# Attention stage of a two-block layer on Trainium2: all scores of a step ahead of the transposes of the step before, and one maximum over three PSUM banks

## The reference

```
def gqa_block(q_blk, k, v):
    s = jnp.einsum('bkgqd,bksd->bkgqs', q_blk, k).astype(jnp.float32) * (HEAD_DIM ** -0.5)
    p = jax.nn.softmax(s, axis=-1)
    return jnp.einsum('bkgqs,bksd->bkgqd', p.astype(v.dtype), v)
...
# first_block: rmsnorm, projection, Fourier branch and attention branch (each gated), output projection, residual, rmsnorm
# second_block: rmsnorm, projections, causal stick-breaking attention, causal convolution, gated merge, then a gated feed-forward part of width 2816
```

## Time and profile before

| what | value |
|---|---|
| median of 3 runs | 2025.19 us |
| the profiled execution | 2023.87 us, its span 2021.9 us |
| PE busy in the span | 1984.7 us (98%) |
| DVE, ACT, POOL busy | 1269.9, 998.3, 771.9 us |
| granted TensorE clock | 0.998 |
| attention stage | from about 262 to about 505 us of the span |
| chain that ended last | 84% PE, 9% DVE, 2% ACT |

### The profile page before, as it was taken

The page is one execution under the profiler, slowest core; times in us unless marked ns, Lnnn a source line. Parts: engine busy times, 40 slices in busy tenths (PEclk is TensorE's granted clock), DMA queues, the critical chain, the costliest instruction groups (busy, mean ns, idle before and its releaser), DMA issues.

```text
span 2021.9 us, 27547 instructions
## 1 busy us (share of the span) xinstructions
PE 1984.7 (98%) x10172; PEld 1653.9 (82%) x10172; DVE 1269.9 (63%) x1892; ACT 998.3 (49%) x1812; POOL 771.9 (38%) x647
## 2 busy tenths in 40 slices
PE   8999999999999999999999999999899999999998
PEld 7888889999777888888888888888788888877886
DVE  5765758888253375766757565089544444449887
ACT  5442259998142364554546532163544444445454
POOL 2332422223333222222223154408987777751000
PEclk9999999999999999999999999999999999999999
DMA  5212120100232121121212353341322222258664
GB/s 161 61 53 73 62 70 12 51 12 10 93 136 75 53 67 49 55 67 57 72 51 94 106 171 122 114 146 53 94 83 73 92 84 73 73 194 269 212 210 172
DMA packets 165438, 190.77 MB, mean 94 GB/s; under 512 B 9243, under 2 KB 115255, under 8 KB 165319
## 3 DMA queue, kind: packets, MB, share of 16 engines
q1 hardware_dynamic: 142743, 133.88, 21.2%
q10 hardware_dynamic: 22576, 55.33, 7.7%
HBM read 148.28 MB, written 40.89 MB: 94 GB/s over the span
## 4 chain that ended last, share of the span: by engine, by line
PE 84%; DVE 9%; issue 2%; ACT 2%; SPq 1%; DMA 1%; POOL 0%; ACTq 0%; DVEq 0%; POOLq 0%
PE psum L1310 18%; PE psum L937 17%; PE psum L939 16%; PE psum L938 16%; PE psum L1206 3%; PE psum L1218 3%; PE psum L1349 2%; PE psum L1237 1%; PE psum L1238 1%; PE psum L1239 1%; PE psum L1366 1%; DVE softplus_part L2640 1%; PE psum L1365 1%; PE psum L1334 1%; PE psum L1333 1%
## 5 line engine op out<-in xcount | busy, mean ns | idle before, releaser
L1310 PE MATMUL psum<-h,w_ring 128*128 128x512 f32 x1728 | 430.6, 399 | 0.7 <-ACT v L1885 0.7
L1310 PEld LDWEIGHTS psum<-h,w_ring 128*128 128x128 f32 x1728 | 314.6, 188 | 67.2 <-ACT v L1885 1.1
L780 POOL TENSOR_TENSOR w_ring<-w_staging,zero 128x8 fp32r<-128x8 f32 x88 | 33.7, 383 | 765.5 <-PE psum L1310 338.1
L783 POOL TENSOR_TENSOR w_ring<-w_staging,w_ring 128x1024 fp32r<-128x1024 f32 (+1 forms) x88 | 223.3, 2538 | 7.3
L2821 DVE TENSOR_TENSOR psum<-psum,product 128x512 f32<-128x512 f32 x80 | 55.7, 698 | 191.3 <-PE psum L939 163.7
L937 PE MATMUL psum<-ffn_in_sums,w_ring 128*128 128x512 f32 x320 | 127.1, 397 | 4.4 <-DVE ffn_in_sums L2795 2.5
L939 PE MATMUL psum<-ffn_in_sums,w_ring 128*128 128x512 f32 x320 | 126.6, 396 | 0.0
L938 PE MATMUL psum<-ffn_in_sums,w_ring 128*128 128x512 f32 x320 | 126.2, 394 | 0.0
L2652 DVE TENSOR_TENSOR stick_w_t<-psum,stick_w_t 128x512 fp32r<-128x512 f32 (+3 forms) x96 | 53.4, 557 | 115.1 <-ACT stick_w_t L1962 114.8
L937 PE MATMUL psum<-w_ring,ffn_split 128*128 128x512 f32 x308 | 122.4, 398 | 0.7 <-POOL w_ring L916 0.6
L939 PE MATMUL psum<-w_ring,ffn_split 128*128 128x512 f32 x308 | 121.9, 396 | 0.0
(11 more groups left out here) (356 smaller groups left out, 5461.9 us busy)
## 6 DMA issues: line engine op xcount, KB each, us to landing
w_staging<-in_w_in SPq DMA_DIRECT2D x57, 512.0 KB, 3.9
w_down_raw<-in_w_down SPq DMA_DIRECT2D x66, 256.0 KB, 3.5
w_staging<-in_w_up SPq DMA_DIRECT2D x24, 512.0 KB, 4.0
w_staging<-scratch_ffn_mid SPq DMA_DIRECT2D x45, 256.0 KB, 3.4
scratch_ffn_mid<-ffn_mid SPq DMA_DIRECT2D x22, 512.0 KB, 2.6
ffn_mid_again<-scratch_ffn_mid SPq DMA_DIRECT2D x43, 256.0 KB, 3.3
w_raw<-in_w_up SPq DMA_DIRECT2D x20, 512.0 KB, 5.2
w_staging<-in_w_out SPq DMA_DIRECT2D x16, 512.0 KB, 3.8
```

The source lines that it names most:

```text
L783: pool.tensor_tensor(lo[:, 0:width], WS[:, s, 0:width], plain(hi[:, 0:width]), ALU.subtract).then_inc(S["w_split"], 1)
L1310: ins = pe.matmul(mix_bank(h), (sl if x == 2 else sh)[:, P * k:P * k + P], ml if x == 1 else mh, start=m == 0, stop=m == UNIT // 2 - 1)
```

## The change

Four things are edited together. PE does all three banks of scores of a step and then all nine turns of the step before; until now the turns of group 0 stood between the second bank and the third. Of the value product, part 0 takes the key tiles 0 to 3 (12 matmuls) and part 1 the tiles 4 to 7 and the meta keys (13). ScalarE does the exponentials of the first two banks in one instruction of 696 elements a partition, then that of the third; `sc_exp` counts two a step, and the scores of the second bank have no wait of their own. The turns of groups 0 and 2 wait for the first exponential of their step and those of group 1 for both. VectorE takes one minimum over the three banks (1044 elements a partition) in place of three instructions, and the semaphore `sc_half` goes.

```diff
             def scores(i, parts=range(3)):
                 h, t = divmod(i, TT)
                 for b in parts:
-                    if i:
-                        pe.wait_ge(S["sc_exp"], 3 * i - 2 + b)
+                    if i and b != 1:
+                        pe.wait_ge(S["sc_exp"], 2 * i - 1 + b // 2)
...
-                    if b:
-                        ins.then_inc(S["sc_half" if b == 1 else "sc_mm"], 1)
+                    if b == 2:
+                        ins.then_inc(S["sc_mm"], 1)
             def turn_probs(i, groups=range(3)):
-                pe.wait_ge(S["sc_exp"], 3 * i + 3)
                 for g in groups:
+                    pe.wait_ge(S["sc_exp"], 2 * i + (2 if g == 1 else 1))
...
+                pe.wait_ge(S["pt_lo"], 6 * p + (6 if part else 4))
                 if part == 0:
-                    pe.wait_ge(S["pt_lo"], 6 * (p + 1))
...
-                for kt in (range(5), range(5, TT))[part]:
+                for kt in (range(4), range(4, TT))[part]:
...
                 if i < HEADS * TT:
-                    scores(i, range(2))
+                    scores(i)
                 if i <= HEADS * TT:
-                    turn_probs(i - 1, range(1))
-                if i < HEADS * TT:
-                    scores(i, range(2, 3))
-                if i <= HEADS * TT:
-                    turn_probs(i - 1, range(1, 3))
+                    turn_probs(i - 1)
...
                 act.wait_ge(S["sc_max"], i + 1)
-                for b in range(3):
-                    act.activation(PR[:, i % 2, KPART * b:KPART * (b + 1)], PB[:, b, 0:KPART], ACT.Exp,
-                                   bias=NB[:, i % 2:i % 2 + 1], scale=-1.0).then_inc(S["sc_exp"], 1)
+                act.activation(PR[:, i % 2, 0:2 * KPART].rearrange("p (b k) -> p b k", k=KPART), PB[:, 0:2, 0:KPART], ACT.Exp,
+                               bias=NB[:, i % 2:i % 2 + 1], scale=-1.0).then_inc(S["sc_exp"], 1)
+                act.activation(PR[:, i % 2, 2 * KPART:KEYS], PB[:, 2, 0:KPART], ACT.Exp,
+                               bias=NB[:, i % 2:i % 2 + 1], scale=-1.0).then_inc(S["sc_exp"], 1)
...
-                first, last = (NB[:, 2 + 2 * (i % 2) + x:3 + 2 * (i % 2) + x] for x in range(2))
-                v.wait_ge(S["sc_half"], i + 1)
-                mark(v.tensor_reduce(first, PB[:, 0:2, 0:KPART], mybir.AxisListType.XY, ALU.min))
                 v.wait_ge(S["sc_mm"], i + 1)
-                link(v.tensor_reduce(last, PB[:, 2, 0:KPART], AX, ALU.min))
-                v.tensor_tensor(NB[:, i % 2:i % 2 + 1], first, last, ALU.min).then_inc(S["sc_max"], 1)
+                v.tensor_reduce(NB[:, i % 2:i % 2 + 1], PB[:, 0:3, 0:KPART], mybir.AxisListType.XY, ALU.min)\
+                 .then_inc(S["sc_max"], 1)
```

More of the change, by code:

```diff
@@ L315 @@
 pr_sq pr_rope pr_t pr_hi pr_done kv_khh kv_kll kv_vhi vv_meta kdup
-sc_half sc_mm sc_max sc_exp pt_mm pt_zero pt_hi pt_lo pt_meta av_mm gate_in0 gate_in1 o_inv o_bank o_out o_hi o_lo
+sc_mm sc_max sc_exp pt_mm pt_zero pt_hi pt_lo pt_meta av_mm gate_in0 gate_in1 o_inv o_bank o_out o_hi o_lo
 mf_in mf_hi mf_done res_in0 res_in1 gains_in x1_out x1_stored
```

## The result

The changed kernel takes 2028.78 us (median of 13 runs, 2027.44 to 2031.41) against 2025.19 us (13 runs as well): a ratio of 1.002, 95% interval 1.0013 to 1.0028, so 3.6 us or 0.18% slower. The forecast was 1.0 us slower. The profiled execution of the changed kernel is one of its longer ones, 2030.61 us, and I compare stages of it, not totals.

The account below looks back on a forecast made before the run. Lopsided attends on PE raised the old 3.557 us step; afterwards an ACT and PE ring of 3.58 binds. 59 steps gave +1.4 us, less 0.24 and 0.14: +1.0, so 2024.9, or 2026.2 us as median; range 2018 to 2032.

Parts of the forecast that it names:

- What bounded the kernel: Attention stage: PE's full busy record hides waiting, some 0.3 us a pair; the mean step is 3.557 us.
- the 3.43 of the old odd step: Old ACT and PE ring where the third exponential was waited for: 1.43 + 0.05 + 0.75 + 0.70 + 0.50 us.
- The parts: Attention step: PE 3.34 us on average, one minimum 1.257 us, wide exponential 0.85 us; even split gives slack, no speed.
- The three rings: Attention step's closed chains: ACT with PE 3.58 us, DVE 3.45, PE 3.34 on average; the longest sets the period.
- The forecast's 3.58: ACT and PE ring per attention step: wide exponential, six scores, four turns, two copies, with links; 3.58 us.
- The sum: Whole kernel: 59 steps x (3.58 - 3.557) = +1.4 us, less 0.24 and 0.14, gives +1.0 us.
- The 0.24 us that step 4 should gain: Stage start: shorter exponentials let step 4 start at most 0.24 us earlier, 0.14 and 0.1 from two steps.
- the faster ones: Two rivals in the attention stage, DVE's pace or an early weight load; results 2018.5 or 2019.7 us, chances 0.12 and 0.06.
- VectorE's ring: Rival: copies don't hold the exponential, the attention stage runs at DVE's 3.45 us; 6.7 us faster, 2018.5; chance 0.12.
- the load isn't ahead: Rival judged: first score's weights load while PE waits, 0.11 us off the ring, 6.5 us off the forecast; chance 0.06.
- The dear exponential: Rival: exponential over two banks costs as two, 0.14 us more a step; 8.3 us above forecast, 2034.5; chance 0.13.
- A small overrun of the ring: Slower case in the attention stage: links add up to 0.06 to 0.1 us more a step; chance 0.06.

Follow-up runs that it names:

- lopsided kernel: The changed kernel with the value product split 15 and 10 again; 2030.32 us against 2025.92 for the kernel before, ratio 1.0025.
- the dosed one: The changed kernel with one added single-column ScalarE copy ahead of the wait for the minimum; 2035.33 us against 2025.92 for the kernel before, ratio 1.005.

## Why the prediction was right, and where it was short

**What bounded the kernel.** Right in the main. PE's full busy record hid waiting. With the uneven split removed the stage ran 0.075 us a step faster. One thing was left out: the 3.43 of the old odd step was put down to ACT and PE alone, but VectorE's minimum ended there at 383.83, 0.03 before the exponential at 383.86, so its ring was as long. It is this ring that stops the old order at about 3.45.

**The parts.** The wide exponential (0.85 forecast, 0.846 measured) and the one maximum (1.257, 1.245) were right to 0.02 us. That both sit differently in the rings was right as well: the exponential's width costs 2.2 us, the maximum nothing. The split gives no speed beside the new order: 0.024 us a step where I had said none.

**The three rings.** Right in which binds. The minimum is ready ahead of the exponential (385.99 against 386.21), lengthening its way by 0.25 moved the short steps by only 0.06 to 0.12, and a small instruction on ACT moved every step. The forecast's 3.58 is the even steps' 3.57. The minimum is 0.16 ahead in the even steps, 0.22 in the plain odd ones and 0.36 in the long ones, where one value, 0.13, was forecast.

**The sum.** This is the step that was too small. I took one ring length for all steps, put together from even-step rows. The term "59 steps x (3.58 - 3.557) = +1.4 us" measured 54 x (3.626 - 3.559) = +3.6 us. Two things were missing. The first is the price of the second wait in odd steps. The earlier trace rows have the odd step's copy 0.75 after the turns' load, and that looks like 0.11 + 0.60 + 0.03 = 0.74 with nothing left over. But a late load delays a turn by less than it does a score, as two records of the kernel before show, the four turns of that step and the nine at the stage's end, which also stood behind a wait:

```profile
381.91 0.66 PE L1218 MATMUL psum<-ident,probs 128*128 128x128 f32 x4
...
498.97 1.20 PE L1218 MATMUL psum<-ident,probs 128*128 128x128 f32 x9 [0.19 <-ACT probs L1838]
```

The four record 0.66 us from the load, where four unhindered ones record 0.60; the nine record 1.20, the unhindered ones of the changed kernel 1.14. So the lag is 0.06; the other 0.06 of the 0.75 was the wait. It costs 27 of the 54 steps 0.06, 1.6 us. The second is the 0.13 of the long steps: 12 x 0.13 = 1.6 us. The even steps' 3.565 is 0.015 below 3.58, which gives back 0.8 us in 54 steps. Together 2.4 us on top of the forecast's pace, where 54 x 0.046 = 2.5 was found.

Both were there before the change as well, its odd distances being 3.43 and 3.56. They cost nothing there, because the next even step took them up: around 340 us its pairs were 3.56 + 3.58 = 7.14, and around 382 us 3.43 + 3.71 = 7.14. PE's attends set the pair, and ACT's delays hid in it. The change made ACT the bound, and its delays came to count.

**The start and the end.** The 0.24 us that step 4 should gain did not come: with six scores ahead of the turns, step 3's exponential is no earlier (283.41 in the lopsided kernel, 283.26 before), and in the profiled execution the low clock took 0.9 us. Behind the stage nothing was to move but by the offset. The profiled execution is 4.9 us behind at step 63 and 6.7 at the end: 1.6 more come in between 1434 and 1442 us, in the second block, where the granted clock is 0.88 from 1420 to 1440 and 0.95 up to 1460, against 0.91 and 1.00 before. The change touches nothing there.

**The rivals.** Neither of the faster ones holds: VectorE's ring doesn't bind, the load isn't ahead. The dear exponential doesn't hold either. A small overrun of the ring, 0.046 us a step, is what happened, and the result lies at 0.18%, just inside the 0.2% that I called the same; the interval reaches to 0.28%, so a true loss of over 0.2% isn't excluded. The 3.6 us are more than three times the 1.0 that was forecast: the ring that binds was found, its two odd-step delays were not.

## What to carry to other kernels

Draw the rings, each chain that closes on itself once a step, before counting busy shares. An edit that takes work off an engine but lengthens its instruction ahead of a waiter (one exponential for two) can make the loop slower, as it did here by 0.041 us a step, and one that only evens out a neighbour's load was the part of this change worth having. And when a change moves the bound to another engine, look at every kind of step of that engine first: its small delays, hidden until then, come with it.

## What the runs showed of the hardware

- A second wait on one ACT instruction cost 0.06 us although it had been met 1.6 us before; standing on an instruction off the ring it cost nothing (steps 3.63 to 3.57, 3.76 to 3.70).
- Behind an ACT copy on partitions 64 to 127, the next ACT instruction that reads SBUF started 0.02 to 0.03 after the one before it had ended, and not 0.12 before that end: the exponential in the changed kernel (0.13 us a long step), the added instruction in the dosed one. The same copy on partitions 0 to 63 did not do this. Why is open.
- The granted clock was lower in a stretch between 281 and 286 us (0.51 in the changed kernel, after PE was busy for 1.77 of 3.40 us) in five of the ten profiled kernels that do all six scores first, and in none of the three with the old order. The lopsided kernel had the same 1.77 and kept 1.00. With one traced execution each, that is a hint and no more.
